# Attention in two layers: transposes, their copies and the outputs move one step behind the exponentials

## What is computed

```python
def gqa_block(q, k, v):
    s = jnp.einsum('bqkgd,bskd->bkgqs', q, k).astype(jnp.float32) * (HEAD_DIM ** -0.5)
    p = jax.nn.softmax(s, axis=-1).astype(v.dtype)
    return jnp.einsum('bkgqs,bskd->bqkgd', p, v)

def diff_block(q, k, v, lam):
    s = jnp.einsum('bqhmd,bshmd->bhmqs', q, k).astype(jnp.float32) * (HEAD_DIM ** -0.5)
    p = jax.nn.softmax(s, axis=-1)
    p = p[:, :, 0] - lam * p[:, :, 1]
    return jnp.einsum('bhqs,bshe->bqhe', p.astype(v.dtype), v)
```

## Time and profile before

| | us |
|---|---|
| median of 3 runs | 2677.24 (2677.05 to 2679.8) |
| the profiled execution | 2680.81, span 2678.9 |
| TensorE busy in the span | 2499.7 (93%) |
| VectorE, ScalarE busy | 1030.6 (38%), 832.5 (31%) |
| attention of the first layer, first to last work | 372.0 to 549.0 |
| attention of the second layer | 1683.0 to 1851.9 |

### The profile page before, as it was taken

The page is one execution under the profiler, slowest core; times in us unless marked ns, Lnnn a source line. Parts: engine busy times, 40 slices in busy tenths (PEclk is TensorE's granted clock), DMA queues, the critical chain, the costliest instruction groups (busy, mean ns, idle before and its releaser), DMA issues. The chain is left out here.

```text
span 2678.9 us, 41961 instructions
## 1 busy us (share of the span) xinstructions
PE 2499.7 (93%) x18638; PEld 2384.5 (89%) x18638; DVE 1030.6 (38%) x1350; ACT 832.5 (31%) x1400; POOL 243.2 (9%) x179
## 2 busy tenths in 40 slices
PE   6888989889998999999999799887999899999998
PEld 5878976689998999999989599666999899999998
DVE  4325646643223422222243454566233342222222
ACT  3523345632112322122135233555222232211220
POOL 1421000000002200000225010000000050000000
PEclk8989999999999999999999899999999999999999
DMA  7233233212221122222221531400222122222222
GB/s 209 88 116 114 67 102 111 72 50 85 79 79 59 54 78 68 77 80 70 70 88 32 171 90 37 131 25 24 72 71 83 60 63 80 75 65 82 79 63 72
DMA packets 281140, 213.62 MB, mean 80 GB/s; under 512 B 9056, under 2 KB 278944, under 8 KB 280960
## 3 DMA queue, kind: packets, MB, share of 16 engines
q1 hardware_dynamic: 274640, 208.10, 25.7%
q10 hardware_dynamic: 5808, 2.17, 0.4%
q0 software_dynamic: 512, 0.66, 0.3%
HBM read 206.46 MB, written 4.46 MB: 79 GB/s over the span
## 5 line engine op out<-in xcount | busy, mean ns | idle before, releaser
L1575 PE MATMUL ps<-hH,low 128*128 128x320 f32 x1824 | 424.1, 314 | 37.4 <-DVEq L2156 18.6
L1575 PEld LDWEIGHTS ps<-hH,low 128*128 128x128 f32 x1824 | 309.9, 191 | 41.6 <-DVEq L2156 19.1
L1575 PE MATMUL ps<-hL,wH 128*128 128x320 f32 x1248 | 289.1, 313 | 0.0
L1575 PE MATMUL ps<-hH,wH 128*128 128x320 f32 x1248 | 288.8, 313 | 0.0
L349 PE MATMUL ps<-wH,hL 128*128 128x256 f32 x720 | 208.2, 289 | 14.7 <-DVEq L948 14.7
L1575 PEld LDWEIGHTS ps<-hL,wH 128*128 128x128 f32 x1248 | 213.8, 192 | 0.0
L1575 PEld LDWEIGHTS ps<-hH,wH 128*128 128x128 f32 x1248 | 212.9, 192 | 0.0
L349 PE MATMUL ps<-wL,hH 128*128 128x256 f32 x720 | 205.5, 285 | 0.0
L349 PE MATMUL ps<-wH,hH 128*128 128x256 f32 x720 | 205.5, 285 | 0.0
L1461 DVE TENSOR_TENSOR wL<-raw,wH 128x1024 fp32r<-128x1024 f32 (+1 forms) x46 | 79.8, 1736 | 287.4 <-ACT wH L1406 286.7
L2177 DVE TENSOR_TENSOR gf<-act,ps 128x640 f32<-128x640 f32 x44 | 36.1, 821 | 372.7 <-PE ps L1575 372.7
(11 more groups left out here) (277 smaller groups left out, 5129.5 us busy)
## 6 DMA issues: line engine op xcount, KB each, us to landing
raw<-in_w_in SPq DMA_DIRECT2D x56, 1024.0 KB, 5.4
raw<-in_w_ffn_in SPq DMA_DIRECT2D x88, 512.0 KB, 5.0
modw<-in_w_mod SPq DMA_DIRECT2D x24, 1024.0 KB, 5.3
gmod<-in_w_mod SPq DMA_DIRECT2D x16, 1024.0 KB, 7.9
raw<-in_w_branch SPq DMA_DIRECT2D x24, 512.0 KB, 3.4
raw<-in_w_ffn_out SPq DMA_DIRECT2D x16, 768.0 KB, 4.9
raw<-in_w_ffn_out SPq DMA_DIRECT2D x16, 640.0 KB, 4.6
head_w<-in_w_mod SPq DMA_DIRECT2D x8, 1024.0 KB, 12.4
```

The lines of the kernel that those rows point to most:

```text
L1575: last = nc.tensor.matmul(m.ps[:, 2 * pair + h, 0:HALF], w[:, k, c * P:(c + 1) * P], a[:, k, h * HALF:(h + 1) * HALF], start=(k == 0 and q ...
```

## The change

All three loops run one iteration longer, i from 0 to S + 1. In iteration i:
- TensorE issues the scores of i+2 as before, and then the chunks of step i-1 (none in iteration 0).
- ScalarE issues the first half of the exponential of i+1, then the first of its copies of step i-1, then the second half, then its other copies of i-1, then the square of step i-3. `exp(s, half)` issues one half; for a context step a half is two of the four instructions. The waits for the maximum and for the turn of step s-3 stand ahead of half 0.
- VectorE weighs step i and takes the maximum of i+2 as before, and then makes its copies of step i-1.
- The splits of the next stage's weights stand in iterations 35 and 36 in the first layer, 28 and 30 in the second, which are with the same steps' chunks as before.

No instruction is added or taken away, no buffer and no semaphore; for a context step `exp_done` now rises by one with each half instead of by two at the end. The same waits guard the same buffers.

```diff
--- before.py
+++ after.py
@@ -1176,19 +1176,20 @@
 
             scores(0)
             scores(1)
-            for s in range(S + 1):
-                if s + 2 < S:
-                    scores(s + 2)
-                for c in of_step[s]:
+            for i in range(S + 2):
+                if i + 2 < S:
+                    scores(i + 2)
+                s = i - 1
+                for c in of_step[s] if i else ():
                     first, n, o, mod, _, _, turn = chunks[c]
                     if c >= 2:
                         pe.wait_ge(*freed(c - 2))
                     if n:
                         parts = parts_of[kind_of[s]]
                         pe.wait_ge(m.sem("e_ready"), e_count[s] + min(parts, (first + n + 4) // 5))
-                        for i in range(n):
-                            b = first + i
-                            last = nc.tensor.transpose(bank(c)[:, i * P:(i + 1) * P], m.e[:, s % 3, b * P:(b + 1) * P],
+                        for j in range(n):
+                            b = first + j
+                            last = nc.tensor.transpose(bank(c)[:, j * P:(j + 1) * P], m.e[:, s % 3, b * P:(b + 1) * P],
                                                        m.cst[:, K_ID:K_ID + P])
                     if o is not None:
                         last = values(o, bank(c)[:, n * P:])
@@ -1212,20 +1213,36 @@
 
         @block.scalar
         def _(act):
-            def exp(s):
-                act.wait_ge(m.sem("maximum"), s + 1)
-                if s >= 3:
-                    act.wait_ge(m.sem("chunk_done"), turned(s - 3))
+            def exp(s, half):
+                if half == 0:
+                    act.wait_ge(m.sem("maximum"), s + 1)
+                    if s >= 3:
+                        act.wait_ge(m.sem("chunk_done"), turned(s - 3))
                 if steps[s][1] < CTX:
-                    for half in range(2):
-                        nc.scalar.activation(m.e[:, s % 3, half * T:(half + 1) * T], both(s)[:, half, :], ACT.Exp,
-                                             bias=m.a_st[:, s, half:half + 1], accum_out=m.a_st[:, s, 2 + half:3 + half]
-                                             ).then_inc(m.sem("exp_done"), 1)
+                    ins = nc.scalar.activation(m.e[:, s % 3, half * T:(half + 1) * T], both(s)[:, half, :], ACT.Exp,
+                                               bias=m.a_st[:, s, half:half + 1], accum_out=m.a_st[:, s, 2 + half:3 + half])
                 else:
-                    for n in range(4):
+                    for n in (2 * half, 2 * half + 1):
                         ins = nc.scalar.activation(m.e[:, s % 3, n * P:(n + 1) * P], quad(s)[:, n // 2, n % 2, :], ACT.Exp,
                                                    bias=quad_st(s)[:, n:n + 1], accum_out=quad_st(s)[:, 4 + n:5 + n])
-                    ins.then_inc(m.sem("exp_done"), 2)
+                ins.then_inc(m.sem("exp_done"), 1)
+
+            def copy(s, c):
+                first, n, o, mod, by, _, _ = chunks[c]
+                if mod is not None:
+                    act.wait_ge(m.sem("slab_used"), mod + 1)
+                    if mod >= 8:
+                        act.wait_ge(m.sem("chunk_done"), done_of(turn_chunk[0]))
+                    nc.scalar.activation(m.mrow[:, mod % 8 // 2, (mod % 2) * W256:(mod % 2 + 1) * W256],
+                                         bank(c)[:, 0:W256], ACT.Copy).then_inc(m.sem("chunk_copied_act"), 1)
+                elif by == "act":
+                    act.wait_ge(m.sem("chunk_done"), done_of(c))
+                    ins = nc.scalar.activation(m.eT[:, s % 2, first:first + n, :].rearrange("p t c -> p (t c)"),
+                                               bank(c)[:, 0:n * P], ACT.Copy)
+                    if o is not None:
+                        _, qt, j = steps[o]
+                        ins = nc.scalar.activation(m.rq[:, j, POS[qt], :], bank(c)[:, n * P:(n + 1) * P], ACT.Copy)
+                    ins.then_inc(m.sem("chunk_copied_act"), 1)
 
             def square(s):
                 kind, qt, j = steps[s]
@@ -1237,32 +1254,23 @@
                     nc.scalar.activation(m.o_sq[:, n % 2, :], m.rq[:, 4 + j + i, qt, :], ACT.Square,
                                          accum_out=m.sml[:, g:g + 1]).then_inc(m.sem("o_squared"), 1)
 
-            exp(0)
-            for s in range(S + 1):
-                if s + 1 < S:
-                    exp(s + 1)
-                for c in of_step[s]:
-                    first, n, o, mod, by, _, _ = chunks[c]
-                    if mod is not None:
-                        act.wait_ge(m.sem("slab_used"), mod + 1)
-                        if mod >= 8:
-                            act.wait_ge(m.sem("chunk_done"), done_of(turn_chunk[0]))
-                        nc.scalar.activation(m.mrow[:, mod % 8 // 2, (mod % 2) * W256:(mod % 2 + 1) * W256],
-                                             bank(c)[:, 0:W256], ACT.Copy).then_inc(m.sem("chunk_copied_act"), 1)
-                    elif by == "act":
-                        act.wait_ge(m.sem("chunk_done"), done_of(c))
-                        ins = nc.scalar.activation(m.eT[:, s % 2, first:first + n, :].rearrange("p t c -> p (t c)"),
-                                                   bank(c)[:, 0:n * P], ACT.Copy)
-                        if o is not None:
-                            _, qt, j = steps[o]
-                            ins = nc.scalar.activation(m.rq[:, j, POS[qt], :], bank(c)[:, n * P:(n + 1) * P], ACT.Copy)
-                        ins.then_inc(m.sem("chunk_copied_act"), 1)
-                if s >= 2 and kind_of[s - 2] in ("diff", "ctx diff"):
-                    square(s - 2)
-                if s == (34 if more else 27):
+            exp(0, 0)
+            exp(0, 1)
+            for i in range(S + 2):
+                own = [c for c in of_step[i - 1] if chunks[c][4] == "act"] if i else []
+                if i + 1 < S:
+                    exp(i + 1, 0)
+                for c in own[:1]:
+                    copy(i - 1, c)
+                if i + 1 < S:
+                    exp(i + 1, 1)
+                for c in own[1:]:
+                    copy(i - 1, c)
+                if i >= 3 and kind_of[i - 3] in ("diff", "ctx diff"):
+                    square(i - 3)
+                if i == (35 if more else 28):
                     next_high(nc, m, act, nxt)
-            if kind_of[S - 1] in ("diff", "ctx diff"):
-                square(S - 1)
+            square(S - 1)
 
         @block.vector
         def _(dve):
@@ -1338,12 +1346,13 @@
 
             maximum(0)
             maximum(1)
-            for s in range(S + 1):
-                if s < S:
-                    weigh(s)
-                if s + 2 < S:
-                    maximum(s + 2)
-                for c in of_step[s]:
+            for i in range(S + 2):
+                if i < S:
+                    weigh(i)
+                if i + 2 < S:
+                    maximum(i + 2)
+                s = i - 1
+                for c in of_step[s] if i else ():
                     first, n, o, mod, by, _, turn = chunks[c]
                     if by == "dve":
                         dve.wait_ge(m.sem("chunk_done"), done_of(c))
@@ -1356,7 +1365,7 @@
                         if o is not None:
                             ins = out(o, bank(c)[:, n * P:])
                         ins.then_inc(m.sem("chunk_copied_dve"), 1)
-                if s == (35 if more else 29):
+                if i == (36 if more else 30):
                     next_low(nc.vector, m, dve, nxt)
             dve.wait_ge(*freed(max(turn_chunk.values())))
             order.step(affine(nc, m, dve, order, L, 1))
```

## The result

| | before | changed |
|---|---|---|
| median | 2677.14 us (2675.01 to 2679.8, 4 runs) | 2647.56 us (2646.15 to 2651.89, 4 runs) |
| ratio | | 0.9885, 95% interval 0.9873 to 0.9898 |
| span of the profiled execution | 2678.9 us | 2650.0 us |
| attention, first layer | 178.30 us | 163.78 us |
| attention, second layer | 170.36 us | 153.22 us |

The account below looks back on a forecast made before the run. TensorE's queue bounds the kernel, idling 22.3 and 28.2 us ahead of transposes. Middles 11.9 + 15.3, drains 2.8 + 2.4 and clock 1.2 + 1.2 give 34.8 us off 2677.2: 2642.5 us, range 2632 to 2661.

Parts of the forecast that it names:

- the wait for the weighing: TensorE ahead of transposes turning a diff step: the wait goes, 10.8 us in the first layer, 16.9 in the second.
- the one ahead of the third chunk: TensorE in gqa turns, waiting for the first chunk's copy: shrinks from 0.77 to 0.49 us each, can't go.
- the beat of 3.40: Shortest time between exponentials in attention: 3.40 us a step, 0.18 above a diff turn without a slab.
- (1): Rival: wait ahead of the third chunk stays at 0.77 us, from two banks or a late first half; 2651; chance 0.17.
- (2): Rival: exponentials' beat binds, first half late in nearly every step, diff turns wait 0.6 us more; 2661; chance 0.12.
- (3): Rival: the two score sets are worked one after the other, steps 5.13 us instead of 4.64; 2710; chance 0.04.
- (4): Rival: waits leave the transposes and return ahead of the scores for the same sum; no change, 2677; chance 0.05.
- The clock's 1.2: TensorE's lower clock after the mid-stream stall and the one in the drain: without these, 1.2 us gained a layer.
- the drain: End of each attention: the last diff step's transposes no longer wait 2.41 us; gain 2.8 us first layer, 2.4 second.
- filling the pipeline: Start of attention: first transposes come after scores 3 instead of 2, step 4's scores end within 0.1 us; costs nothing.
- ScalarE's split: Second layer, mid-stream: ScalarE's half of splitting the next stage's weights costs about 0.7 us.
- VectorE's: Second layer, mid-stream: VectorE's split of the next weights makes the maximum 1.1 us late beyond its slack, instead of 3.33 idle.

Follow-up runs that it names:

- one added copy a step: Changed kernel plus one dead 128x512 ScalarE copy ahead of each exponential's first half, in 28 iterations a layer: 2647.43 us.
- the lag alone: Changed kernel with chunks still one step behind, but ScalarE issuing both exponential halves before its copies, as in the kernel before: 2650.37 us.
- two more copies: Changed kernel plus two dead 128x512 ScalarE copies ahead of each exponential's first half, in 28 iterations a layer: 2661.92 us.

## Why the prediction was right, and where it missed

**Direction, mechanism, range: right.** 2647.56 lies in 2632 to 2661, and both waits did what was said: the wait for the weighing is gone, and the one ahead of the third chunk fell to 0.49. The prices of the layout were found again: the beat of 3.40 and the third chunk 1.34 behind the first. The rivals fell by number: the bubble is 0.49 and not 0.77 (1); one added copy a step is nearly free (2); the steps became shorter and not 0.49 us longer (3); the waits that came back ahead of the scores are 3.0 and 5.4 us, a small part (4).

**The two gains weren't separate.** The sum puts 31 x 0.28 = 8.7 us down to the shorter wait ahead of third chunks, by the copy between the halves, and takes 3.1 off for the beat (1.2 and 1.9; 11 x 0.18 is 2.0, though). Against the kernel before that gain is there. But the lag alone has the whole gain of the steady part already (198.11 against 198.17 us): its third chunks wait 0.67 and not 0.77, and without the copy between the halves the diff turns pay nothing for the beat. So the total came out near for both parts together, while the second part, as made here, was worth nothing there.

**Size: 3.8 us short.** 34.8 us were forecast within attention; the means of all profiles are 347.9 before (two) and 316.9 changed (three), 31.0. By the median the gain is 29.6. I cut both stages at the third chunks of step 2 and step 31, and count the scores that the changed kernel has issued by then (1.28 more) to the same side. The forecast is cut in the same places: of its middle, 0.87 and 1.10 us are waits ahead of the cut at step 2, and 2.07 in the second layer (1.12 for the weighing, 1.44 - 0.49 for a copy) stand behind step 31. The clock's 1.2 is counted to the drain in the first layer and to the middle in the second, where the stalls stood. Means of all profiles:

| stretch | first layer, gain us | forecast | second layer, gain us | forecast |
|---|---|---|---|---|
| filling, up to step 2 | 0.1 | 0.9 | 0.5 | 1.1 |
| middle, step 2 to 31 | 10.9 | 11.0 | 13.0 | 13.3 |
| drain, behind step 31 | 3.4 | 4.0 | 3.1 | 4.5 |

- **Two steps of the sum excluded each other.** I said that filling the pipeline moves nothing, and still took the waits within it (0.87 in the first layer, 0.86 and 0.24 in the second) as gained, as part of the 22.3 and 28.2 us. Its stretch takes 17.7 to 19.3 us before (with the 1.28) and 17.7 to 18.9 changed, so filling moved nothing that can be told from this scatter. That is 2.0 us too much in the sum.
- **The drain was read from before alone.** I took its waits away and put none in. Without scores in front, the transposes of the last diff step wait 0.58 us for VectorE to free their bank, in both layers, and in the second one the third chunk of the last full gqa step waits for a copy that now stands behind half of a context step's four exponentials, 1.06 us instead of 0.49:

```profile
526.33 0.14 PEld L1192 LDWEIGHTS ps<-cst,e 128*128 128x128 f32 x1 [0.58 <-DVE rq L1340]
...
1812.90 0.61 ACT L1240 ACTIVATE eT<-ps 128x512 f32<-128x512 f32 x1
1813.57 0.20 PEld L1192 LDWEIGHTS ps<-cst,e 128*128 128x128 f32 x2 [1.06 <-ACT eT L1240]
```

  That is 0.58 x 2 + 0.57 = 1.7 us, of the 2.0 that the drain is short. By the table filling is short by 1.4 us, the middle by 0.4 and the drain by 2.0; with profiles of one kernel 1.5 us apart, the split is good to about 1 us.
- **ScalarE's split** cost 1.53 - 0.35 = 1.2 us, not 0.7. VectorE's was right (1.15 for 1.1). The size of the clock's term, 1.2 us a layer, no run shows by itself.
- **The page's rule.** By the Trainium skill (Perfetto Trace Analysis, § Identifying Performance Opportunities) a gap that repeats can mean too little PSUM. Here, at the same two banks, the lag took 0.10 of the 0.77 us, the order on ScalarE 0.18 and three blocks in the first chunk 0.11, so the trace agrees at most for what is left; whether a third bank takes that, no run here shows.

**A version that is at least as fast.** The copy between the halves only in gqa turns gave 2641.56 and 2643.76 us. Against the changed kernel it is 2.1 to 6.0 us less, with intervals that overlap; its steady part is 3.5 us shorter in both profiles.

## What to carry to other kernels

When a queue in program order waits each round for a result that was started in the same round, one round of lag can be worth the whole wait, as here; lay out one round from durations, with each handoff, and look for the first moment at which another engine must be free. An order within the round is worth far less: in every turn it gave nothing in the steady part, since it moved the wait from one kind of turn to the other, and 3.5 us where only the turns that gain got it. Test each part of a change alone, and compare stretches that repeat from profile to profile, not the span. Then do the filling and the draining by hand as well: waits there must not be counted with the steady ones, and the drain has waits of its own that the steady rounds hide.

## What the runs showed of the hardware

The granted clock falls for a longer or a shorter time in stretches of the same work. From the third chunk of step 15 to that of step 18 in the first layer, TensorE also runs the 32 tiny matmuls of a modulation turn. The first profile of the changed kernel and the one for its comparison anew, then the two profiles of the kernel before (columns as above):

```profile
443.47:461.07 17.60, 17.35 (x148) 13.73 (x148) 9.19 (x18) 8.35 (x25) 0.45 (x1) 0.90 0.26 81
```

```profile
437.82:456.95 19.13, 18.88 (x147) 15.13 (x147) 9.19 (x18) 8.35 (x25) 0.46 (x1) 0.82 0.22 74
```

```profile
445.42:464.60 19.18, 18.93 (x147) 15.30 (x147) 8.76 (x17) 8.18 (x27) 0.45 (x1) 0.82 0.24 74
```

```profile
446.37:463.95 17.58, 17.33 (x148) 13.71 (x148) 8.76 (x17) 8.18 (x27) 0.46 (x1) 0.90 0.25 80
```

1.5 and 1.6 us lie between two profiles of one and the same kernel, with the clock at 0.82 or 0.90 of full on average: it is at the lower of its two levels for a longer or a shorter part. Of the 14 profiles eight have 17.5 to 17.6 us here, one (two more copies) 17.8 and five 19.1 to 19.3, in old and new orders alike. In the second layer the stretch with the turn (step 22 to 27) takes 24.3 to 24.7 us in seven profiles of kernels with the lag, 22.7 to 22.9 in three and 25.3 with two more copies. Where no tiny matmuls and no stall stand, in the steady stretches of the changed kernel, the clock is 1.00 and three profiles agree within 0.02 us. Outside, filling differs by up to 1.6 us between profiles of one kernel, and the first attention of the changed kernel began at 372.1, 374.1 and 367.5 us. So the spans of single profiles of one kernel differ by 3 to 7 us without a cause in the code, and the time of a steady stretch, next to its waits, tells more than the span does.
